# Attention probabilities turned in 32x32 squares by VectorE in place of TensorE transposes, in a two-block fp32 transformer on one core

## The reference, cut to what matters

```python
p = jax.nn.softmax(logits, axis=-1)          # rows: queries, columns: keys
return jnp.einsum('bhqs,bshd->bqhd', p, v)   # sums over keys
```

## Time and profile before

| what | value |
|---|---|
| median of 3 runs | 2922.37 us (2922.26 to 2922.62) |
| the profiled execution's own time | 2922.03 us |
| its span | 2920.2 us |
| TensorE, VectorE, ScalarE busy | 2898.1, 1906.7, 1363.7 us |
| granted TensorE clock | 1.00 |

### The profile page before, as it was taken

The page is one execution under the profiler, slowest core; times in us unless marked ns, Lnnn a source line. Parts: engine busy times, 40 slices in busy tenths (PEclk is TensorE's granted clock), DMA queues, the critical chain, the costliest instruction groups (busy, mean ns, idle before and its releaser), DMA issues.

```text
span 2920.2 us, 33076 instructions
## 1 busy us (share of the span) xinstructions
PE 2898.1 (99%) x13622; PEld 2420.9 (83%) x13622; DVE 1906.7 (65%) x2448; ACT 1363.7 (47%) x1755; POOL 61.9 (2%) x108
## 2 busy tenths in 40 slices
PE   8999999999999999999999999999999999999999
PEld 8998788888887888888888888888888888888887
DVE  5666675669877674577785544555897667457664
ACT  5545544444554443444446555444444444344443
POOL 1000000000011000000001000000000000000000
PEclk9999999999999999999999999999999999999999
DMA  7455555555566555555555445555555555555554
GB/s 267 158 185 183 178 184 180 199 202 189 204 245 221 200 193 196 189 200 188 190 200 195 160 172 184 171 178 194 192 199 195 194 190 199 188 197 191 189 200 159
DMA packets 84103, 561.76 MB, mean 192 GB/s; under 512 B 10067, under 2 KB 10211, under 8 KB 19056
## 3 DMA queue, kind: packets, MB, share of 16 engines
q1 hardware_dynamic: 77760, 544.80, 54.4%
q0 software_dynamic: 3456, 10.01, 1.2%
q10 hardware_dynamic: 2736, 4.83, 0.6%
HBM read 557.50 MB, written 3.68 MB: 192 GB/s over the span
## 4 chain that ended last, share of the span: by engine, by line
PE 98%; DVE 1%; ACT 0%; DMA 0%; issue 0%; DVEq 0%; ACTq 0%
PE acc L620 95%; PE misc L620 2%; PE misc L624 1%; DVE w_lo L1410 1%; DMA xT<-in_xT 0%; ACT w_hi L986 0%; DMA lam_vec<-in_lam_vectors 0%; ACT prob L965 0%; DVE lru_work L1662 0%; ACT u_hi L968 0%; DVE turned L1410 0%; DVE prob L1416 0%; ACT L965 0%; ACT av L968 0%; DVE y_lru_lo L1410 0%
## 5 line engine op out<-in xcount | busy, mean ns | idle before, releaser
L1410 DVE TENSOR_TENSOR w_lo<-raw,w_hi 128x1024 fp32r<-128x1024 f32 x1032 | 1256.5, 1220 | 837.4 <-ACT w_hi L986 830.9
L986 ACT ACTIVATE w_hi<-raw 128x1024 fp32r<-128x1024 f32 x1032 | 1087.4, 1056 | 1240.2 <-PE acc L620 1239.2
L620 PE MATMUL acc<-w_hi,v_hi 128*128 128x512 f32 x1408 | 548.1, 389 | 0.0
L620 PE MATMUL acc<-w_hi,v_lo 128*128 128x512 f32 x1408 | 547.8, 389 | 0.0
L620 PE MATMUL acc<-w_lo,v_hi 128*128 128x512 f32 x1408 | 547.7, 389 | 0.0
L620 PE MATMUL acc<-w_hi,u_hi 128*128 128x512 f32 (+1 forms) x1248 | 493.2, 395 | 0.0
L620 PE MATMUL acc<-w_hi,u_lo 128*128 128x512 f32 (+1 forms) x1248 | 483.3, 387 | 0.0
L620 PE MATMUL acc<-w_lo,u_hi 128*128 128x512 f32 (+1 forms) x1248 | 482.6, 387 | 0.0
L620 PEld LDWEIGHTS acc<-w_hi,v_hi 128*128 128x128 f32 x1408 | 264.3, 188 | 57.4 <-issue 2.6
L620 PEld LDWEIGHTS acc<-w_hi,v_lo 128*128 128x128 f32 x1408 | 264.3, 188 | 54.8
L620 PEld LDWEIGHTS acc<-w_lo,v_hi 128*128 128x128 f32 x1408 | 264.3, 188 | 54.7
(11 more groups left out here) (310 smaller groups left out, 2956.7 us busy)
## 6 DMA issues: line engine op xcount, KB each, us to landing
raw<-in_w_gates SPq DMA_DIRECT2D x112, 1024.0 KB, 4.9
raw<-in_w_ffn_gate SPq DMA_DIRECT2D x88, 1024.0 KB, 4.8
raw<-in_w_ffn_up SPq DMA_DIRECT2D x88, 1024.0 KB, 4.8
raw<-in_w_ffn_down SPq DMA_DIRECT2D x88, 1024.0 KB, 4.8
raw<-in_w_in SPq DMA_DIRECT2D x67, 1024.0 KB, 4.8
raw<-in_w_out SPq DMA_DIRECT2D x32, 1024.0 KB, 4.8
raw<-in_w_branch SPq DMA_DIRECT2D x24, 1024.0 KB, 4.8
raw<-in_w_mem SPq DMA_DIRECT2D x8, 1024.0 KB, 4.9
```

What stands on the lines that cost most here:

```text
L620: return e.matmul(o, w, x, start=start, stop=stop, skip_group_check=True)
L986: e.activation(m.w_hi[:, n % PART_SLOTS, 0:HALF_KT * cols], m.raw[:, c % RAW_SLOTS, o * cols:(o + HALF_KT) * cols], ACT.Copy).then_inc(s[" ...
L1410: return e.tensor_tensor(o, a, b, op)
```

## The change

Four of the five attentions (differential, forgetting, both dense ones, dilated; the window attention stays) no longer use TensorE to turn probabilities. VectorE turns them in SBUF with 16 square transposes a head in two steps of eight. Each instruction reads 32 partitions and the same 32 columns of all tiles: 32x96 elements for three tiles, 32x128 for four, 32x192 for six. The PSUM bank and the copy out of it go. Av waits for `turned` on VectorE. It stays in step 6 for dense heads and step 8 for dilated tiles, and moves from step 5 to step 6 in differential and forgetting heads, which so take one step more. The loop of `moved` becomes a function of its own, with the same instructions. The diff is cut to its core; the ScalarE hunks left out only replace a step's bank and yields by the same number of steps, or one more in differential and forgetting heads.

```diff
@@ -171,23 +171,23 @@
                 "decay2", "loss", "loss_abs", "cube1", "cube2", "cube3", "drive", "half_drive", "scan", "gelu",
                 "y", "y_lo")
 LRU_ACT = Steps("e", "gate0", "gate1", "gate2", "gate3", "exp", "tanh_half", "tanh", "root", "gelu_tanh", "y_hi")
-DIFF_PE = Steps("scores", "turn", "av", "turn_y")
-DIFF_DVE = Steps("logits0", "logits1", "max0", "max1", "inv0", "inv1", "inv_lam", "p0", "p", "copy", "normed", "y_lo",
+DIFF_PE = Steps("scores", "av", "turn_y")
+DIFF_DVE = Steps("logits0", "logits1", "max0", "max1", "inv0", "inv1", "inv_lam", "p0", "p", "turned", "normed", "y_lo",
                  head=("prod0", "sum0", "prod1", "sum1", "lam_diff", "lam", "gain"))
 DIFF_ACT = Steps("exp0", "exp1", "copy", "y_hi", head=("lam",))
 WIN_PE = Steps("scores", "turn0", "turn1", "av", head=("turn_dk",))
 WIN_DVE = Steps("logits0", "logits1", "max0", "max1", "floor0", "floor1", "sum0", "sum1", "inv0", "inv1", "copy0",
                 "copy1", "y_lo", head=("neg_sink", "dk"))
 WIN_ACT = Steps("exp0", "sink0", "exp1", "sink1", "p0", "p1", "y_hi")
-FOX_PE = Steps("scores", "turn", "av", head=("turn_cf",))
-FOX_DVE = Steps("max", "inv", "copy", "y_lo", head=("f", "neg", "e", *LOG1P, "floor", "log", "sums", "terms"))
+FOX_PE = Steps("scores", "av", head=("turn_cf",))
+FOX_DVE = Steps("max", "inv", "turned", "y_lo", head=("f", "neg", "e", *LOG1P, "floor", "log", "sums", "terms"))
 FOX_ACT = Steps("exp", "p", "y_hi", head=("e",))
-DENSE_PE = Steps("scores", "turn", "av")
-DENSE_DVE = Steps("max", "inv", "y_lo")
-DENSE_ACT = Steps("exp", "p", "copy", "y_hi")
-DIL_PE = Steps("scores0", "scores1", "scores2", "turn0", "turn1", "av")
-DIL_DVE = Steps("add0", "add1", "add2", "max", "inv", "p", "y_lo")
-DIL_ACT = Steps("exp", "copy0", "copy1", "y_hi")
+DENSE_PE = Steps("scores", "av")
+DENSE_DVE = Steps("max", "inv", "turned", "y_lo")
+DENSE_ACT = Steps("exp", "p", "y_hi")
+DIL_PE = Steps("scores0", "scores1", "scores2", "av")
+DIL_DVE = Steps("add0", "add1", "add2", "max", "inv", "p", "turned", "y_lo")
+DIL_ACT = Steps("exp", "y_hi")
 ROTATE = Steps("lo_a", "lo_b", "lo", "hi_a", "hi_b", "hi")
 HEAD_RUNS = {"kc": [("kc", 0, 0, 4)], "qc": [("qc", 0, 0, 4)], "qb": [("qb", 0, 0, 4)],
              "kb": [("qb", 4, 0, 2), ("kb", 0, 2, 4)], "a0": [("qa", 0, 0, 4)],
@@ -577,7 +577,7 @@
     for i in range(4):
         hh, qt = divmod(i, 2)
         if i >= 2:
-            e.wait_ge(s["dil_pe"], DIL_PE("turn1", i - 2))
+            e.wait_ge(s["dil_dve"], DIL_DVE("turned", i - 2))
         for g in range(3):
             rows = dram["scratch_bias"][2 * g + hh]
             skew = bass.AP(rows.tensor, rows.offset + 255 - P * qt, [[BW - 1, P], [1, SEQ]])
@@ -727,15 +727,10 @@
             paired_scores([bank for _, bank in banks], m.aqT[:, h, :], m.akT[:, h, :], "diff_pe")
             for n in range(2):
                 bank_free[banks[n][0]] = ("diff_dve", DIFF_DVE(f"logits{n}", h))
-            yield 4
-            i, bank = task_bank()
-            need(("diff_dve", DIFF_DVE("p", h)))
-            transposes(bank, [tile(m.prob[0], n) for n in range(3)], "diff_pe")
-            bank_free[i] = ("diff_dve", DIFF_DVE("copy", h))
-            yield
+            yield 6
             i, bank = task_bank()
             need(freed(plan["keep4"]))
-            need(("diff_dve", DIFF_DVE("copy", h)))
+            need(("diff_dve", DIFF_DVE("turned", h)))
             pT, hs = m.probT[h % 2], slice(h * P, (h + 1) * P)
             matmul(bank[:, 0:P], tile(pT, 0), m.av[:, 0, hs], True, True)
             matmul(bank[:, P:SEQ], tile(pT, 1), m.av[:, 0, hs], False, False)
@@ -801,15 +796,10 @@
 
             banded_scores(bank, m.cqT[:, h, :], m.ckT[:, h, :], "fox_pe", extra)
             bank_free[i] = ("fox_act", FOX_ACT("exp", h))
-            yield 4
-            i, bank = task_bank()
-            need(("fox_act", FOX_ACT("p", h)))
-            transposes(bank, [tile(m.prob[h % 2], n) for n in range(3)], "fox_pe")
-            bank_free[i] = ("fox_dve", FOX_DVE("copy", h))
-            yield
+            yield 6
             i, bank = task_bank()
             need(freed(plan["keep8"]))
-            need(("fox_dve", FOX_DVE("copy", h)))
+            need(("fox_dve", FOX_DVE("turned", h)))
             banded_av(bank, m.cv, m.probT[h % 2], slice(h * P, (h + 1) * P)).then_inc(s["fox_pe"], 1)
             bank_free[i] = ready["y_fox", h] = ("fox_dve", FOX_DVE("y_lo", h))
             lanes.wrote("y_fox", [h])
@@ -895,15 +885,9 @@
                             m.dest[keys][:, kv, :], qt == 0)
             mm.then_inc(s[f"{name}_pe"], 1)
             bank_free[i] = (f"{name}_act", DENSE_ACT("exp", h))
-            yield 4
+            yield 6
             i, bank = task_bank()
-            need((f"{name}_act", DENSE_ACT("p", h)))
-            transposes(bank, [m.prob2[h % 2][:, qt, st * P:(st + 1) * P] for st in range(2) for qt in range(2)],
-                       f"{name}_pe")
-            bank_free[i] = (f"{name}_act", DENSE_ACT("copy", h))
-            yield 2
-            i, bank = task_bank()
-            need((f"{name}_act", DENSE_ACT("copy", h)))
+            need((f"{name}_dve", DENSE_DVE("turned", h)))
             matmul(bank[:, 0:SEQ], v[:, 0, kv * P:(kv + 1) * P], m.prob2T[h % 2][:, 0, :], True, False)
             matmul(bank[:, 0:SEQ], v[:, 1, kv * P:(kv + 1) * P], m.prob2T[h % 2][:, 1, :], False, True).then_inc(
                 s[f"{name}_pe"], 1)
@@ -926,16 +910,9 @@
                        m.dest["ka"][:, 2 * g + hh, :]).then_inc(s["dil_pe"], 1)
                 bank_free[i] = ("dil_dve", DIL_DVE(f"add{g}", n))
                 yield
-            yield 4
-            for half in range(2):
-                i, bank = task_bank()
-                need(("dil_dve", DIL_DVE("p", n)))
-                flat = m.probd[n % 2][:, :, :].rearrange("p a b -> p (a b)")
-                transposes(bank, [tile(flat, 3 * half + a) for a in range(3)], "dil_pe")
-                bank_free[i] = ("dil_act", DIL_ACT(f"copy{half}", n))
-            yield
+            yield 5
             i, bank = task_bank()
-            need(("dil_act", DIL_ACT("copy1", n)))
+            need(("dil_dve", DIL_DVE("turned", n)))
             need(freed(plan["in2_3"]))
             need(freed(plan["in2_4"]))
             for a in range(6):
@@ -1226,9 +1201,7 @@
             yield 2
             e.wait_ge(s["fox_dve"], FOX_DVE("inv", h))
             normalise(m.prob[h % 2], m.attn[h % 2], "fox_act")
-            yield
-            task_bank()
-            yield
+            yield 3
             bank = task_bank()
             e.wait_ge(s["fox_pe"], FOX_PE("av", h))
             activate(m.left["y_fox"][0][:, h, :], bank[:, 0:SEQ], ACT.Copy).then_inc(s["fox_act"], 1)
@@ -1346,12 +1319,7 @@
             for qt in range(2):
                 i = scaled(p[:, qt, :], p[:, qt, :], stat[:, 2 + qt:3 + qt])
             i.then_inc(s[f"{name}_act"], 1)
-            yield
-            bank = task_bank()
-            yield
-            e.wait_ge(s[f"{name}_pe"], DENSE_PE("turn", h))
-            scaled(pT[:, :, :], bank[:, :].rearrange("p (a b) -> p a b", a=2), 1.0).then_inc(s[f"{name}_act"], 1)
-            yield
+            yield 3
             bank = task_bank()
             yield
             e.wait_ge(s[f"{name}_pe"], DENSE_PE("av", h))
@@ -1374,12 +1341,7 @@
             yield
             e.wait_ge(s["dil_dve"], DIL_DVE("max", n))
             activate(flat, flat, ACT.Exp, bias=stat[:, 0:1], accum_out=stat[:, 2:3]).then_inc(s["dil_act"], 1)
-            yield 3
-            for half in range(2):
-                bank = task_bank()
-                e.wait_ge(s["dil_pe"], DIL_PE(f"turn{half}", n))
-                scaled(turned[:, 384 * half:384 * (half + 1)], bank[:, 0:384], 1.0).then_inc(s["dil_act"], 1)
-            yield
+            yield 4
             bank = task_bank()
             yield
             e.wait_ge(s["dil_pe"], DIL_PE("av", n))
@@ -1499,19 +1461,33 @@
             stt(sig[:, 0, :], sig[:, 0, :], half_r2[:, 0:1], v[:, 0, :], ALU.mult, ALU.mult)
             stt(sig[:, 1, :], sig[:, 1, :], half_r2[:, 1:2], v[:, 1, :], ALU.mult, ALU.mult).then_inc(freed, 1)
 
-    def moved(left, j, tokens, turned, gain=None):
+    def turn_squares(tokens, turned, steps, done):
 
 
         squares = tokens.rearrange("p t (m n b) -> p t m n b", m=4, n=4)
         to = turned[:, :, :].rearrange("p m (t i b) -> p t m i b", t=2, i=4)
-        per_step = 16 // turn_steps(j, left)
         for n in range(16):
             i, f = divmod(n, 4)
             mm = e.transpose(to[32 * f:32 * f + 32, :, :, i, :], squares[32 * i:32 * i + 32, :, :, f, :])
             if n == 15:
-                mm.then_inc(s["moved_turned"], 1)
-            if (n + 1) % per_step == 0:
+                mm.then_inc(s[done], 1)
+            if (n + 1) % (16 // steps) == 0:
                 yield
+
+    def turn_tiles(tiles, turned, done):
+
+        for n in range(16):
+            i, f = divmod(n, 4)
```

(40 more changed lines are left out.)

## The result

The changed kernel takes 2939.07 us (median of 4 runs, 2938.67 to 2939.89), the kernel before 2922.49 us on the same chip (4 runs, 2922.26 to 2922.68). The ratio is 1.0055 with a 95% interval of 1.0043 to 1.0067: slower by 16.6 us. The profiled execution took 2938.67 us, its span is 2936.8 us. The forecast was +7.2 us: right in sign and inside the range, but less than half the loss.

A forecast was written before the change was run, and what follows sets the result against it. TensorE, busy 99% of the span, was taken to bound the kernel. New waits of 16.9 us less 9.7 saved gave +7.2 us on 2922.0, a median of 2929.6 us, 0.25% slower; range 2918 to 2941.

The forecast's parts named there:

- What goes, 88 x 0.11 = 9.7 us: TensorE loses 88 transposes at 0.11 us each in the chain, a gross gain of 9.7 us.
- Rival 2: TensorE's transposes cost their recorded 272 ns, so 23.9 us go and the kernel takes 2915.4 us; chance 0.06.
- Removed copies and VectorE's load at nothing: ScalarE's 18 and VectorE's eight removed copies gain nothing; VectorE's 110 us of extra work is hidden as throughput.
- Prices of the squares: VectorE's squares take 0.278, 0.312 and 0.379 us for 96, 128 and 192 columns, from the slope of tensor_tensor.
- Rival 1: Squares are cheaper and av's wait in dense and dilated heads vanishes, most likely near 2922 us; chance 0.20.
- rival 3: More collisions with evacuations, 2939 us, or squares at 0.445 us for every width, 2980 us; chance 0.14.
- Dense and dilated waits: TensorE waits for squares before av: 7.2 us over the dense heads, 6.2 us over four dilated tiles.
- 7.00 us against 7.54. TensorE waits 0.54 us: Dense gqa head: TensorE reaches av 7.00 us after VectorE's step-4 split starts, the squares end after 7.54.
- Differential: Head 0 waits 3.7 us in place of 1.5, 2.2 more; head 1 does not wait, heads 2 and 3 near zero.
- Forgetting: Heads have 7.01 us against 6.98; the second meets a branch evacuation and waits 1.3 us; added steps cost nothing.
- POOL's fetch of the skewed bias: Dilated tiles: POOL fetches some 4 us later, after VectorE's turned tile, covered by 25 us, so no wait.
- The pace of 0.445 us: VectorE's pace for existing 256-column squares, read from four and the following gap, 637.68 to 639.48: they do not overlap.

The follow-up runs named there:

- Experiment 7: Changed kernel with av one step later in all heads and all 16 squares in the first of the two steps: 2911.04 us, ratio 0.9962.
- Experiment 3: Kernel before, transposes kept, with 224 squares added on VectorE in dense heads and dilated tiles, nothing waiting for them: 2922.58 us, ratio 0.9999.
- Experiment 4: Kernel before with 16 added squares in each dense head and dilated tile, for which TensorE waits before av: 2933.95 us, ratio 1.0038.
- experiment 2: Changed kernel with all 16 squares in the first of the two steps, av where it is: 2918.77 us, ratio 0.9985.
- experiment 5: Changed kernel with av one step later in the dense heads and dilated tiles only: 2920.5 us, ratio 0.9992.
- experiment 9: Changed kernel with av one step later, window attention's 24 transposes also replaced by squares in two steps, its av in step 9: 2913.23 us, ratio 0.9967.
- experiment 8: Kernel before with 20 added squares in each dense head and dilated tile, for which TensorE waits before av: 2955.89 us, ratio 1.0114.

## Why the prediction was right in sign and 9.4 us short

- **What goes, 88 x 0.11 = 9.7 us: right.** Experiment 7, where nothing waits for squares, gains 11.4 us against the 11.4 that the transposes, the old wait of head 0 and its restart make. Rival 2 (their recorded 272 ns, 23.9 us) falls. The Trainium skill, "TensorE: Matmul & The Clock Gate", Part 4: PE-mode transpose, has about 275 ns for one transpose in a kernel's context; the recorded duration agrees (271), but in this stream it is not what a transpose costs.
- **Removed copies and VectorE's load at nothing: right.** Experiment 3 adds 70 us of squares for nothing; that the removed copies are worth nothing no run tests alone, but experiment 7's sum needs no term for them. VectorE's wait for ScalarE shrank by 78 us (830.9 to 753.3), not by the forecast 106.
- **Prices of the squares: right.** Eight take 2.50 us (128 columns) and 3.04 (192), 0.31 and 0.38 each, as the slope of tensor_tensor gave. The chains came out at 7.44 and 8.51 us for 7.54 and 8.60. Rival 1 needed them 27 ns cheaper; it falls. The upper end of rival 3 falls too.
- **Dense and dilated waits: right place, too small.** The forecast had 7.2 and 6.2 us, TensorE's matmuls stood 9.3 and 6.6. The step that failed is "7.00 us against 7.54. TensorE waits 0.54 us": it takes the end of the last square as the end of the wait, and the wait as its whole price. Behind it come 0.14 us to TensorE's start and 0.24 us of restart.
- **Differential: the wait right, its price not.** Head 0 waits 3.9 us (forecast 3.7), and no term had the fall of the clock behind it, 1.5 us. Heads 1 and 3 do not wait; head 2 has a wait of 0.4 us of the weight load, and a restart.
- **Forgetting: half right.** The second head met the branch's evacuation as counted, visible above at 461.32 and 462.64; TensorE's matmuls wait 1.5 us for 1.3. The others were given no wait, and their weight loads wait 0.4, 1.2 and 0.5 us. The forecast had "no slack left" there, and the hand-off turns that into the 0.4 and 0.5. The third head is another matter: the first eight squares hold up VectorE's evacuation of the gate, ScalarE waits for that and gets to its next half of a split late. ScalarE's timeline:

```profile
491.23 1.06 ACT L942 ACTIVATE gate<-gate 128x1024 f32<-128x1024 f32 x1 [2.21 <-DVE gate L1378]
492.20 1.04 ACT L963 ACTIVATE w_hi<-raw 128x1024 fp32r<-128x1024 f32 x1
```

  The split of VectorE and its second eight squares stand behind it (from 494.53), and av starts at 496.93. This is read from the trace alone; no run took it apart.
- **POOL's fetch of the skewed bias: right.** It waits for VectorE's turned tile now, and TensorE never for it.
- **Two slips in its numbers.** The pace of 0.445 us leaves the gap out; with it, 637.68 to 639.48 is 1.80 us, 0.45 each. And at rival 3's upper end (0.445 for every width) the chains of the ten dense heads grow by 2.1 us, not 2.7, so that end is some 44 us, not 50. Neither touches the forecast.

**The sum again.** TensorE stands 22.1 us for squares (forecast 7.2 + 6.2 + 3.7 + 1.3 = 18.4). Two terms no forecast had: ten dense heads, four tiles and six others restart, 20 x 0.24 = 4.8 us, and the clock behind head 0 costs 1.5. Less 1.5 for the old wait, 0.2 for its restart and 9.7 for the transposes makes 17.0, with the 0.5 us of the kernel's start, whose cause stays open, 17.5: 0.9 more than the 16.6 measured. Most of that excess lies in the second block, where the rows make 12.3 us (15.9 idle, 3.4 restarts, less 7.0) and the split starts 11.5; it stays open too. So of the 9.4 us by which the forecast was short, about 4.6 are restarts, 3.7 longer waits (the hand-offs of 0.14 us, less what the trains came out shorter, and the forgetting heads), 1.5 the clock and 0.5 the start; these add up to 10.3, and the 0.9 left open is the difference. The mechanism held: which engine waits for which, where, and in the dense, dilated and differential heads for how long, within a few tenths of a microsecond. The price behind each wait was missing.

## What to carry to other kernels

When work moves off the engine that sets the time to an in-order helper, its idle share says only that the load fits; what decides is the chain on the helper from its last fixed point to the consumer, with everything queued between, against the consumer's own way there. Price each new wait as its length and the hand-off and the restart (here 0.14 and 0.24 us), so that even a wait of nearly nothing, twenty times over, is several microseconds. Look at the granted clock behind the longest waits too: a mean of 0.999 over the span hid a fall that cost 1.5 us. Then let the consumer come one step later, or keep the helper's steps together: with the same instructions that turned 16.6 us lost into 11 won.

## What the runs showed of the hardware that was not expected

- A wait of TensorE in a dense stream of matmuls costs 0.24 us beyond its length, by the chain: 1.10 for 0.86 us, 1.57 for 1.34, 0.91 for 0.67, with 4, 12 and 6 matmuls behind it. Of the 0.24, 0.16 us is the overlap with the matmul ahead that the stream has, and 0.08 longer records (1.10 for 1.02). Experiment 4 bears it out as a sum (14 x 0.24 = 3.4 us over the idle time). It was not measured in a kernel of its own.
- Where the wait was long, the granted clock fell from 2.4 to 1.2 GHz behind it, for 3 us or more: after 3.9 us of standing in the changed kernel, 2.9 in experiment 2, 4.1 in experiment 5, 2.06 in experiment 9 and 2.48 in two tiles of experiment 8. After waits of 2.48 and 2.53 us in that run's other two tiles, and of 2.50 in its first dense head, it did not fall. Each fall cost 1.3 to 2.3 us more by the rows.
- The time from VectorE's last square to TensorE's matmul was 0.14 and 0.15 us in the two kinds of heads read above.
- A square transpose of f32 costs a fixed part and about 1 ns a column: 269, 302 and 369 ns for 96, 128 and 192 columns, 436 for 256, and the next one starts only after it (eight of 128 columns take 2.50 us).
